# Attention in one decoder layer: values as the stationary operand, probabilities streaming in two column groups, and the division moved behind the pass

## What is computed

```python
def sparse_softmax(q, kg, vg, valid):                 # q: 8 heads of 64; kg, vg: the selected keys and values
    logits = einsum('bqhd,bqkhd->bqhk', q, kg) * (HEAD_DIM ** -0.5)
    logits = where(valid[:, :, None, :], logits, -inf)
    p = softmax(logits, axis=-1)
    return einsum('bqhk,bqkhd->bqhd', p, vg)

def trunk_layer(x, ...):
    ...
    attn = attend(q, k, v, qi, wi, ki).reshape(B, T, ATTN_DIM)      # ATTN_DIM = 512, selection by an indexer's top-k
    conv_out = cb * causal_dwconv(u_hist, conv_w)                   # 512 channels
    mixed = sigmoid(ga) * (attn @ w_o_attn) + sigmoid(gc) * (conv_out @ w_o_conv)
    h = x + mixed @ w_merge
    ...
```

## Time and profile before

| | |
|---|---|
| three executions, median (range) | 1732.44 us (1731.13 to 1738.52) |
| the profiled execution: its own time | 1742.39 us |
| its span in the profile | 1740.5 us |
| mean granted TensorE clock | 0.982 |
| TensorE matmuls (PE) busy | 1668.0 us, 96% of the span |
| TensorE weight loads (PEld) busy | 1592.3 us, 91% |
| VectorE (DVE) busy | 1219.4 us, 70% |
| ScalarE (ACT) busy | 661.4 us, 38% |
| GpSimd (POOL) busy | 799.9 us, 46% |

### The profile page before, as it was taken

The page is one execution under the profiler, slowest core; times in us unless marked ns, Lnnn a source line. Parts: engine busy times, 40 slices in busy tenths (PEclk is TensorE's granted clock), DMA queues, the critical chain, the costliest instruction groups (busy, mean ns, idle before and its releaser), DMA issues.

```text
span 1740.5 us, 31401 instructions
## 1 busy us (share of the span) xinstructions
PE 1668.0 (96%) x11555; PEld 1592.3 (91%) x11555; DVE 1219.4 (70%) x1897; ACT 661.4 (38%) x997; POOL 799.9 (46%) x402
## 2 busy tenths in 40 slices
PE   7989999999999989999899998999999999999999
PEld 5958899999999877777899998899999999999999
DVE  5669999999899844545543477867777775655555
ACT  4764643223211276665211344443444444211110
POOL 2504771445786622330212216666666666643331
PEclk9999999999999889999999999999999999999999
DMA  5221112111776333323333312222212222522222
GB/s 198 75 80 37 37 49 87 62 49 61 242 228 204 115 110 98 97 69 123 114 126 144 122 61 97 86 73 72 85 72 75 94 72 97 220 97 97 97 78 97
DMA packets 66979, 178.34 MB, mean 102 GB/s; under 512 B 15386, under 2 KB 15514, under 8 KB 66762
## 3 DMA queue, kind: packets, MB, share of 16 engines
q1 hardware_dynamic: 56786, 140.91, 24.1%
q10 hardware_dynamic: 9392, 32.10, 4.9%
q0 software_dynamic: 720, 4.29, 0.6%
HBM read 141.79 MB, written 35.58 MB: 102 GB/s over the span
## 4 chain that ended last, share of the span: by engine, by line
PE 74%; DVE 13%; ACT 4%; issue 3%; POOL 3%; DMA 2%; SPq 0%; DVEq 0%; ACTq 0%; POOLq 0%
PE PS L660 17%; PE PS L1078 15%; PE PS L1142 11%; PE PX L1078 6%; PE PS L1000 5%; PE PS L1046 5%; PE PX L1142 4%; DVE S L2135 2%; PE PS L948 2%; DVE M L2133 2%; PE PS L918 2%; PE PX L931 2%; DVE LD L2115 2%; DVE PB L2172 1%; PE PS L980 1%
## 5 line engine op out<-in xcount | busy, mean ns | idle before, releaser
L660 PE MATMUL PS<-XH,WHI 128*128 128x346 f32 (+1 forms) x984 | 321.0, 326 | 6.3 <-POOL WLO L1769 5.0
L660 PE MATMUL PS<-XL,WHI 128*128 128x346 f32 (+1 forms) x984 | 317.8, 323 | 0.0
L660 PE MATMUL PS<-XH,WLO 128*128 128x346 f32 (+1 forms) x984 | 317.0, 322 | 0.0
L1769 POOL TENSOR_TENSOR WLO<-WRAW,WHI 128x1024 fp32r<-128x1024 f32 x58 | 143.6, 2477 | 329.3 <-ACT WHI L1170 329.2
L2135 DVE MATCH_REPLACE8 S<-M,S 128x1024 f32<-128x1024 f32 (+3 forms) x224 | 206.2, 928 | 0.0
L2133 DVE MAX8 M<-S 128x8 f32<-128x1024 f32 (+3 forms) x224 | 201.0, 933 | 0.4
L660 PEld LDWEIGHTS PS<-XH,WHI 128*128 128x128 f32 x984 | 186.2, 189 | 16.2 <-issue 9.5
L660 PEld LDWEIGHTS PS<-XH,WLO 128*128 128x128 f32 x984 | 186.4, 189 | 0.0
L660 PEld LDWEIGHTS PS<-XL,WHI 128*128 128x128 f32 x984 | 186.2, 189 | 0.0
L2391 DVE TENSOR_TENSOR HY<-HY,PS 128x344 f32<-128x344 f32 x198 | 100.9, 514 | 79.2 <-PE PS L1142 79.2
L1142 PE MATMUL PS<-FH,DLO 128*128 128x344 f32 x396 | 126.7, 320 | 0.0
(11 more groups left out here) (363 smaller groups left out, 4573.5 us busy)
## 6 DMA issues: line engine op xcount, KB each, us to landing
WRAW<-wtiles SPq DMA_DIRECT2D x49, 512.0 KB, 3.6
KR<-cache_k SPq DMA_DIRECT2D x64, 256.0 KB, 3.0
RING<-cache_v SPq DMA_DIRECT2D x64, 256.0 KB, 2.9
ffn_act<-TG ACTq DMA_DIRECT2D x22, 516.0 KB, 2.7
FRAW<-ffn_act SPq DMA_DIRECT2D x11, 1032.0 KB, 7.0
RAWG<-wtiles SPq DMA_DIRECT2D x22, 512.0 KB, 3.6
RAWV<-wtiles SPq DMA_DIRECT2D x22, 512.0 KB, 4.3
DRAW<-wdown SPq DMA_DIRECT2D x11, 1024.0 KB, 4.9
```

Source lines behind the costliest of these rows:

```text
L660: last = nc.tensor.matmul(PS[b][:, c, 0:n], w[b][:, kk, :], x[:, kk, t0 + c * n:t0 + (c + 1) * n], start=(kk == 0 and p == 0), stop=(kk == ...
L1769: nc.gpsimd.tensor_tensor(WLO[b][:, :, :], WRAW[b][:, :, :], WHI[b][:, :, :].bitcast(F32), ALU.subtract).then_inc(w_lo[b], 1)
```

## The change

- **Product with the values.** The operands change places: the 64 value columns are the stationary operand, and the transposed probabilities stream, 128 columns a tile. The output has features on partitions, 64 rows. Successive key tiles use alternate halves of the output partitions (and of the array's columns), chosen by `g = 64 * ((kt + e + 1) % 2)`, and each half is accumulated by itself. `out` on VectorE copies one half to `AO` (128 features of a pair by tokens) and adds the other. The final transposes and `AT` are gone.
- **Order.** `qk(u+3)` stands ahead of `turn(u+1)`, except where its block is the widest (1056 keys). `PB` has three buffers, since logits for unit u+3 may now be written before unit u+1 is transposed.
- **Division.** ScalarE's row sums go to `SUMQ`, one column per unit. After a pass VectorE takes 18 reciprocals at once. For passes 0 to 2, SyncE writes these 128x18 elements to DRAM (`sums`), waits for that, and loads them back, each head's row broadcast over its 64 partitions, into `RS2`; GpSimd multiplies the pair's tile `AO[:, i-1, :]` (128x1048) by it at unit 3 of the next pass. For the last pass TensorE spreads the reciprocals over partitions with 18 matmuls against the identity, and VectorE multiplies.
- **High and low parts.** In the last pass ScalarE rounds the three divided tiles to `AH` after units 4, 7 and 10 (`SPLIT`), and GpSimd subtracts for `AL`. 
- **End of the stage.** The first output tile now begins with the attention products of the three finished pairs (27 matmuls), goes on with the convolution part, k tile by k tile (36), and ends with the last pair (9). The scaling of `OD` moves into the third and fourth pass. The zero columns of `AH` and `AL` behind column T are no longer written.

```diff
-        PB = [at(f"PB{b}", [P, TP], 97920 + b * R) for b in range(2)]
+        PB = [at(f"PB{b}", [P, TP], o) for b, o in enumerate((97920, 97920 + R, 172736))]
...
-        AT = at("AT", [P, NB, 512], 183232)
+        AO = at("AO", [P, 4, TP], 183232)
+        RS2 = at("RS2", [P, NB * P], 172736 + R)
+        SUMQ = at("SUMQ", [P, 4 * 18], 168640)
...
-        px_out = [t[:, 2, 32:32 + HD] for t in PS]
...
+        px_out = [t[:, 2, 32:32 + P] for t in PS]
+        px_dec = [t[:, 2, 160:416] for t in PS]
...
+        sums_d = nc.dram_tensor("sums", (3, 2, NB * P), F32, kind="Internal").ap()
...
+        SPLIT = (4, 7, 10)
+        FIRSTS = [x for x, (b, e) in enumerate(UNITS) if KT_N[b] > 1]
...
-                sp.wait_ge(a_pv, NU * (i - 1) + VALUES[1] + 1 + FREE)
+                sp.wait_ge(a_pv, NU * (i - 1) + VALUES[-1] + 1 + FREE)
...
+                sp.wait_ge(a_rc, i)
+                sp.dma_start(sums_d[i - 1].rearrange("e (b q) -> q e b", b=NB), SUMQ[:, NU * (i - 1):NU * i].rearrange("q (e b) -> q e b", e=2),
+                             allow_slow_non_contiguous=True).then_inc(s_io, 16)
+                sp.wait_ge(s_io, 48 * (i - 1) + 16)
+                if i > 1:
+                    sp.wait_ge(a_norm, i - 1)
+                for e in range(2):
+                    sp.dma_start(RS2[e * HD:(e + 1) * HD, :], sums_d[i - 1, e:e + 1, :].to_broadcast([HD, NB * P])).then_inc(s_io, 16)
...
-                for kt in range(KT_N[b]):
-                    w = min(P, S_W[b] - kt * P)
-                    v = VLAST[:, e * HD:(e + 1) * HD] if kt == 8 else VT[0:w, kt, ds(i * P + e * HD, HD)]
-                    last = nc.tensor.matmul(px_out[u % 2][0:ROWS[b], :], PTB[u % 2][0:w, kt, 0:ROWS[b]], v,
-                                            start=(kt == 0), stop=(kt == KT_N[b] - 1))
+                n, r = KT_N[b], ROWS[b]
+                for kt in range(n):
+                    w, g = min(P, S_W[b] - kt * P), HD * ((kt + e + 1) % 2)
+                    v = VLAST[:, e * HD:(e + 1) * HD] if kt == 8 else VT[0:w, kt, i * P + e * HD:i * P + (e + 1) * HD]
+                    last = nc.tensor.matmul(px_out[u % 2][g:g + HD, 0:r], v, PTB[u % 2][0:w, kt, 0:r], start=(kt < 2), stop=(kt >= n - 2))
...
+                    wide = S_W[UNITS[(u + 3) % NU][0]] > 1024
+                    if more(u + 3) and not wide:
+                        qk(u + 3, i)
                     if more(u + 1):
                         turn(u + 1, i)
-                    if more(u + 3):
+                    if more(u + 3) and wide:
                         qk(u + 3, i)
                     pv(u, i, extra)
...
+            def out_chunk(b, q, c, k0=0, k1=4):
+                xh, xl = ((AH, AL), (COH, COL))[q]
+                for kk in range(k0, k1):
+                    for p, (w, x) in enumerate(((WHI, xh), (WHI, xl), (WLO, xh))):
+                        last = nc.tensor.matmul(PS[q][:, c, 0:CW], w[b][:, 4 * q + kk, :], x[:, kk, C0 + c * CW:C0 + (c + 1) * CW],
+                                                start=(kk == 0 and p == 0), stop=(kk == 3 and p == 2))
+                return last
...
-            pe.wait_ge(a_o, 4 * NU + FREE)
-            for t in range(NB):
-                if t >= 4:
-                    pe.wait_ge(at_l, t - 3)
...
-                    out_part(1, 1)
-            pe.wait_ge(at_l, NB + 1)
-            out_part(1, 0).then_inc(mm[1], 1)
+            def spread(b):
+
+                dst = PX[1][:, 0:LR] if b == 8 else PS[1][:, b // 4, b % 4 * P:(b % 4 + 1) * P]
+                for e in range(2):
+                    last = nc.tensor.matmul(dst[e * HD:(e + 1) * HD, :],
+                                            SUMQ[0:ROWS[b], 3 * NU + NB * e + b:3 * NU + NB * e + b + 1].to_broadcast([ROWS[b], HD]),
+                                            CK[0:ROWS[b], C_ID:C_ID + ROWS[b]], start=True, stop=True)
+                return last
+
+            pe.wait_ge(a_rc, 4)
+            pe.wait_ge(a_ta, 4 * NBAT + FREE)
+            for b in range(NB):
+                last = spread(b)
+            last.then_inc(d_at, 1)
+            pe.wait_ge(d_o, 2)
...
+            pe.wait_ge(w_lo[1], 22)
+            pe.wait_ge(at_h, 3)
+            pe.wait_ge(at_lp, 3)
+            for c in range(2):
+                out_chunk(1, 0, c, 0, 3)
+            pe.wait_ge(at_l, 1)
+            out_chunk(1, 0, 2, 0, 3)
+            pe.wait_ge(a_norm, 4)
+            for kk, (done, n) in enumerate(((co_l, 1), (co_l, 2), (co_lp, 1), (co_l, 3))):
+                pe.wait_ge(done, n)
+                for c in range(NCH):
+                    out_chunk(1, 1, c, kk, kk + 1)
+            pe.wait_ge(at_l, 2)
+            for c in range(NCH):
+                last = out_chunk(1, 0, c, 3, 4)
+            last.then_inc(mm[1], 1)
...
-                nc.scalar.activation(PB[u % 2][0:ROWS[b], 0:S_W[b]], PB[u % 2][0:ROWS[b], 0:S_W[b]], ACT.Exp,
+                nc.scalar.activation(PB[u % 3][0:ROWS[b], 0:S_W[b]], PB[u % 3][0:ROWS[b], 0:S_W[b]], ACT.Exp,
                                      bias=SM[0:ROWS[b], 18 + u:19 + u], scale=HD ** -0.5,
-                                     accum_out=SM[0:ROWS[b], 36 + u:37 + u]).then_inc(a_exp, 1)
+                                     accum_out=SUMQ[0:ROWS[b], ds(NU * i + NB * e + b, 1)]).then_inc(a_exp, 1)
...
+            def attention_high(j):
+
+                act.wait_ge(a_norm, j + 1)
+                if j == 0:
+                    act.wait_ge(k_saved, 16)
+                nc.scalar.copy(AH[:, j, 0:TPR], AO[:, j, 0:TPR]).then_inc(at_h, 1)
...
+                    if last and u in SPLIT:
+                        attention_high(SPLIT.index(u))
...
+            step(nc.scalar.copy(SUMQ[:, :], CK[:, C_ONES:C_ONES + 4 * NU]))
...
-            act.wait_ge(a_o, 4 * NU + FREE)
-            act.wait_ge(k_saved, 16)
+            act.wait_ge(d_at, 2)
+            nc.scalar.copy(AH[:, :, TPR:T], PX[0][:, 0:32].rearrange("p (j t) -> p j t", j=4)).then_inc(at_h, 1)
...
             for j in range(4):
+                if j == 2:
+                    act.wait_ge(a_norm, 4)
+                    nc.scalar.copy(AH[:, 3, 0:TPR], AO[:, 3, 0:TPR]).then_inc(at_h, 1)
...
-            for t in range(NB):
-                act.wait_ge(at_t, t + 1)
-                w = P if t < 8 else NMETA
-                nc.scalar.copy(AH[:, :, t * P:t * P + w],
-                               at_banks[t % 4][:, :].rearrange("p (j t) -> p j t", j=4)[:, :, 0:w]).then_inc(at_h, 1)
...
+                    if u == 3 and not (isinstance(i, int) and i == 0):
+                        pool.wait_ge(s_io, 48 * i)
+                        pool.wait_ge(a_o, NU * i + FREE)
+                        pool.sem_inc(held, 1)
+                        nc.gpsimd.tensor_tensor(AO[:, ds(i - 1, 1), 0:T].rearrange("p a t -> p (a t)"),
+                                                AO[:, ds(i - 1, 1), 0:T].rearrange("p a t -> p (a t)"), RS2[:, 0:T],
+                                                ALU.mult).then_inc(a_norm, 1)
...
+                    if last and u - 1 in SPLIT:
+                        j = SPLIT.index(u - 1)
+                        pool.wait_ge(at_h, j + 1)
+                        nc.gpsimd.tensor_tensor(AL[:, j, 0:TPR], AO[:, j, 0:TPR], AH[:, j, 0:TPR].bitcast(F32),
+                                                ALU.subtract).then_inc(at_lp, 1)
...
+                before = BATCHES[(u - 3) % NU][-1][0] + 1
+                dve.wait_ge(a_tm, NBAT * (i + 1) + before if u >= 3 else NBAT * i + before)
...
+            def divide_values(q):
+
+                nc.vector.scalar_tensor_tensor(out=OD[q][:, :], in0=OD[q][:, :], scalar=SM[:, 58 + q:59 + q],
+                                               in1=CK[:, C_BD:C_BD + 512], op0=ALU.mult, op1=ALU.mult).then_inc(d_o, 1)
...
+            def recips(i):
+
+                dve.wait_ge(a_exp, NU * (i + 1))
+                nc.vector.reciprocal(SUMQ[:, NU * i:NU * (i + 1)], SUMQ[:, NU * i:NU * (i + 1)]).then_inc(a_rc, 1)
...
             def out(u, i):
                 b, e = UNITS[u]
                 r = ROWS[b]
...
-                nc.vector.reciprocal(SM[0:r, 36 + u:37 + u], SM[0:r, 36 + u:37 + u]).then_inc(a_rc, 1)
...
+                dst, px = AO[e * HD:(e + 1) * HD, i, b * P:b * P + r], px_out[u % 2]
                 dve.wait_ge(a_pv, NU * i + u + 1 + FREE)
-                ins = nc.vector.tensor_scalar(AT[0:r, b, ds(i * P + e * HD, HD)], px_out[u % 2][0:r, :],
-                                              SM[0:r, 36 + u:37 + u], None, ALU.mult)
...
+                ins = nc.vector.tensor_copy(dst, px[(1 - e) * HD:(2 - e) * HD, 0:r])
+                if KT_N[b] > 1:
+                    ins.then_inc(a_first, 1)
+                    dve.wait_ge(a_first, 16 * i + FIRSTS.index(u) + 1)
+                    ins = nc.vector.tensor_tensor(dst, dst, px[e * HD:(e + 1) * HD, 0:r], ALU.add)
...
+                    if last and u == NU - 1:
+                        recips(i)
...
+                    elif i > 0:
```

(20 more changed lines are left out.)

91 lines of the change are left out of this document (28 added, 63 removed).

## The result

Seven executions of the changed kernel took 1741.88 to 1748.14 us, median **1746.36**; the kernel before, seven executions beside it, 1733.51. The ratio is 1.0053 (95% interval 1.0036 to 1.0070): slower by half a per cent. The prediction, 1706 with a range up to 1730, was wrong. The first profiled execution of the kernel before stood some 9 us above its median, so the two profiled spans (1740.5 and 1744.5 us) differ by less than the medians do.

The account below looks back on a forecast made before the run. TensorE's instructions plus some waits were taken to bound each attention pass. The terms, 29.3 - 15.7 + 3.3 + 10.4 - 1 = 26.3 us off 1742.39, gave 1716.1, or 1706 us on the median's scale; range 1688 to 1730.

Parts of the forecast that it names:

- division's sum: Division between passes: element write L taken as 5 us, then broadcasts and GpSimd's multiplication; a loss of 1 us in all.
- slow element write: Rival: the write of 2304 single elements is slow, up to 30.6 us, making the kernel 1773.8 us; chance 0.12.
- 3 L - 23.1: Waits for the division in the three later passes together, L being the element write's time; slower kernel beyond L = 16.8.
- logits ahead: Next-but-two logits ahead of transposes on TensorE cover waits for exponentials: gain 3.3 us, bounds 0 and 6.6.
- 24-query units: Product with the values in units of 24 queries: loads keep their number, no gain taken, bounds 0 and 4 us.
- Streaming: Product with values stationary in two column groups: 320 x 0.111 = 35.5 us instead of 64.8, gain 29.3 us.
- change of shape: TensorE switching between narrower products and transposes or logits: 0.14 us each, loss 15.7 us, bounds 11.2 and 22.
- Loads beside running matmuls: In the product, weight loads pass running matmuls on the same rows; rival with no overlap 1734.5 or 1798 us, chance 0.04.
- The stage's end: From last product to first output tile: 16.9 us against 27.3, gain 10.4, bounds 8 (a stretch at 1.2 GHz) and 11.5.
- Division on VectorE and GpSimd: VectorE's extra 2 to 4 us per pass stays hidden; GpSimd's multiplication beside VectorE costs nothing.
- ScalarE as the pace: Rival: ScalarE's exponentials and copies set the passes' pace, the 16.9 us saved there become waits, 1723 us; chance 0.14.
- range's good end: 18 us less, 1688: cheap shape changes, no exponential waits, 24-query gain of 4, clock holding 2.4 GHz (some 6 us).

Follow-up runs that it names:

- fast write: The changed kernel, whole division kept, but TensorE transposes the reciprocals and the write to DRAM is 18 rows of 512 bytes: 1709.94 us (0.9821); again 1707.21 (0.9829).
- row write: The changed kernel with the sums written as 128 whole rows of 72 bytes, so in wrong order in DRAM: 1708.73 us, 0.9829 of the kernel before.
- one group: All key tiles in the same half of the columns: on the changed kernel 1743.90 us (1.0040), on it with sums written in whole rows 1719.42 (0.9884).
- three variants: Each against the changed kernel: TensorE's old order 1742.90 us, all key tiles in one column half 1743.90, both heads' values stationary at 128 columns 1743.27.

## Why the prediction was wrong

**The step that failed** is one number of the division's sum: "I take 5, near the first, because nothing suggests that batches exclude each other". The estimate counted the packets' share of the engines and their landing, 4.4 us, and the packets were indeed through in 3.1 to 3.4; but the wait is for the completion, 12.9 to 15.2 us after the issue. That is the rival of the slow element write, to which I gave 0.12, and it was the one on the other side.

**Its price was too small as well.** By its formula, 3 L - 23.1, the mean of 14.1 costs 19 us and leaves the kernel some 8 us faster, with the turning point at 16.8. The waits alone were 22.6, since the splits needed 44.9 us and not 27.6 + 14.2 = 41.8 (an issue one us later, broadcasts 0.8 longer, gaps of 0.4 between GpSimd's instructions), and the 13.9 us of work at a lower clock were not in the sum at all. Taking the single elements away gave back 36 to 39 us.

**The other terms held in their sum.** With the fast write the kernel is 28 to 31 us faster than before; the forecast's sum without the division's 1 us was 27.3. That it agrees so well is partly chance: the logits ahead gave 5 us more than their term and the 24-query units 3.4 that were counted as nothing, while the passes came out shorter than forecast by 4 us only (208.4 to 187.4 with the row write, 21.1 where 16.9 were forecast). One by one:

- *Streaming.* The forecast was 0.111 us for 128 columns in two groups and 0.14 for a change of shape. A product of eight key tiles and the logits behind it:

```profile
634.70 1.09 PE L962 MATMUL PS<-PTB,VT 128*64 128x128 f32 x16
635.72 0.33 PE L931 MATMUL PS<-HKH,HQ 128*128 128x128 f32 x1
```

  1.02 us from start to start, which is 8 x 0.109 + 0.15. The units with 24 queries, for which I took nothing, also gained: 16 of their records take 0.58 us from start to start in the last pass (839.55 to 840.13), where 16 took 1.00 in the last pass before (820.20 to 821.20): 3.4 us in eight units, near the upper bound of 4.
- *Loads beside running matmuls.* In that row every step of 0.109 us holds one record of either group, mostly 36 ns apart there and 6 or 7 ns in most other products; the sixteen loads, 0.13 to 0.14 us each, are through in 0.88 us, beside matmuls on the same 128 rows. So the rule of the Trainium skill that a load overlaps only in another row group ("TensorE: Matmul & The Clock Gate", "Part 3: Packing small matmuls — row/col tiling") does not hold for these column groups.
- *Logits ahead:* 3.3 forecast, 8.6 measured with the row write.
- *The stage's end:* 16.9 forecast, 17.0 measured in the windows.
- *Division on VectorE and GpSimd:* hidden, as forecast. GpSimd's multiplication takes 2.4 us beside VectorE, and VectorE's copy, 0.284 us in the median before, has 0.285 and at most 0.294.
- *ScalarE as the pace:* partly. With the fast write 8.0 us of waits for its copies are left, and with one group there are 2.3; the price I gave, 17 us, was too high.

**The clock** was in the range's good end, as a stretch that might improve, and in the lower bound of the stage's end. In the changed kernel it went the other way: 0.85 over the passes, 0.93 before. Without the element write the traces show 0.94 (row write), 0.89 and 0.95 (fast write), about as before, and a version that hardly waits (one group with the row write) 0.99. That shorter products lower the clock because TensorE reaches its waits sooner fits these numbers, but no run isolates it. The Trainium skill has the pattern ("TensorE: Matmul & The Clock Gate", section "HAM oscillation — how this bites in real kernels": repeated stops for data let the clock fall again after each); the rows around the three long stops agree (0.50 for 4.6 to 6.4 us of work behind each). Whether the smaller dips around the 24-query units come from the stop in front of them stays open, since filling it raised the clock a little but gained no time that two kernels side by side could show.

## What to carry to other kernels

Cost a transfer that others wait for by its completion, not by the packets it moves: here single elements of 4 bytes cost some 6 us more than rows even when there were only 256 of them, while one small transpose on TensorE turned them into whole rows and gave 36 us back. While one wait paced by another queue is left, changes on the waiting engine price nothing (three variants came out alike); take that wait out first, then compare. And when an engine gets faster, add to the price of each new stop the work that it then does at the lower clock.

## What the runs showed of the hardware

- A write to DRAM of 2304 single 4-byte elements ends long after its last packet: the packets were through in 3.4 of 14.6 us. Four value pages behind such a write landed in 13.3 us in the median, instead of 3.
- Two column groups of 64 run beside each other: pairs of records 6 to 36 ns apart, a step every 0.109 us, with the weight loads inside it.
- TensorE's clock differs between executions of one kernel: 0.978 to 0.986 in the mean for the fast write, 11.5 us between its slowest and fastest execution.
